# Decoder layer with 32 experts on one core: another expert's gate kept in the spare buffer, and a rebuilt end

## The reference

```python
def moe_ffn(h, w_router, b_router, w_e_gate, b_e_gate, w_e_up, b_e_up, w_e_down, b_e_down):
    ...
    combine = jnp.sum(jax.nn.one_hot(top_idx, N_EXPERTS) * top_w[..., None], axis=1)   # top 4 of 32

    def expert_step(acc, args):
        wg, bg, wu, bu, wd, bd, cw = args
        g = jnp.minimum(xt @ wg + bg, SWIGLU_LIMIT)
        u = jnp.clip(xt @ wu + bu, -SWIGLU_LIMIT, SWIGLU_LIMIT)
        y = ((u + 1.0) * g * jax.nn.sigmoid(SWIGLU_ALPHA * g)) @ wd + bd
        return acc + cw[:, None] * y, None
    ...
x = x + y @ w_out
x = x + moe_ffn(rms_norm(x, g_mlp), ...)
return x
```

## Time and profile before

| | before |
|---|---|
| median of 3 runs | 1132.2 us |
| profiled execution, its own time | 1131.85 us |
| its span, first to last instruction | 1129.9 us |
| PE busy | 1073.4 us (95%) |
| DVE busy | 452.4 us (40%) |
| ACT busy | 170.7 us (15%) |
| POOL busy | 90.1 us (8%) |
| read from HBM | 438.38 MB |
| DMA rate over the span | 389 GB/s |
| weights loaded, expert matrices in full | 4096 KB each, 28.5 to 31.1 us from issue to landing |

### The profile page before, as it was taken

One profiled execution on the slowest core, in us unless ns is written; L12 is line 12 of the kernel. 1 busy time (PEld: TensorE's weight loads), 2 busy tenths in 40 slices (PEclk: granted clock), 3 DMA queues, 4 the chain that ended last, 5 costly groups with the idle time before them and its releaser, 6 DMA issues.

```text
span 1129.9 us, 14464 instructions
## 1 busy us (share of the span) xinstructions
PE 1073.4 (95%) x5719; PEld 510.5 (45%) x5719; DVE 452.4 (40%) x1070; ACT 170.7 (15%) x342; POOL 90.1 (8%) x89
## 2 busy tenths in 40 slices
PE   9999999999999998989889999999899999899998
PEld 7779899843333333333333333333333333233333
DVE  5883666533333333333333333333333233333333
ACT  7546655300000000000000000000000000000000
POOL 3227446000000000000000000000000000000000
PEclk9999999999999999999999999999999999999999
DMA  9836424999999999999999999999999999999996
GB/s 382 361 149 253 195 76 171 421 422 430 427 431 429 432 434 428 432 432 435 427 429 432 430 433 426 431 431 427 431 431 430 427 431 429 431 427 428 427 423 259
DMA packets 27536, 440.09 MB, mean 389 GB/s; under 512 B 3009, under 2 KB 4418, under 8 KB 6114
## 3 DMA queue, kind: packets, MB, share of 16 engines
q1 hardware_dynamic: 26752, 438.71, 91.5%
q10 hardware_dynamic: 738, 0.73, 0.2%
HBM read 438.38 MB, written 1.05 MB: 389 GB/s over the span
## 4 chain that ended last, share of the span: by engine, by line
PE 67%; DMA 30%; DVE 1%; ACT 1%; issue 0%; POOL 0%; DVEq 0%; POOLq 0%
PE bank L1936 40%; DMA ring<-in_w_e_up_dram 30%; PE bank L1901 3%; PE bank L1958 2%; PE bank L1691 1%; PE bank L1921 1%; PE bank L1692 1%; PE bank L1693 1%; PE bank L1980 1%; PE bank L1536 1%; PE bank L1960 1%; PE bank L1778 1%; PE bank L1545 1%; PE bank L1737 1%; PE bank L1779 1%; PE bank L1780 1%
## 5 line engine op out<-in xcount | busy, mean ns | idle before, releaser
L1936 PE MATMUL bank<-ring,heads 128*64 128x512 f32 x3004 | 690.8, 606 | 0.2 <-DVE heads L1335 0.2
L1936 PEld LDWEIGHTS bank<-ring,heads 128*64 128x64 f32 x3004 | 204.0, 138 | 388.4 <-issue 387.8
L1474 DVE TENSOR_TENSOR x<-x,bank 128x512 f32<-128x512 f32 x124 | 79.6, 683 | 145.9 <-PE bank L1960 145.9
L925 ACT ACTIVATE heads<-heads 128x512 f32<-128x512 f32 x32 | 20.2, 630 | 669.6 <-DVE heads L1407 669.6
L1444 DVE SCALAR_TENSOR_TENSOR y_lo<-bank,small,y_hi 128x512 fp32r<-128x512 f32 x31 | 23.3, 750 | 212.5 <-ACT y_hi L921 212.5
L1921 PE MATMUL bank<-bias_parts,e_sel 128*128 128x512 f32 x63 | 32.6, 518 | 46.4 <-DMA ring<-in_w_e_up_dram 42.8
L728 POOL TENSOR_TENSOR x<-x,heads 128x256 f32<-128x256 f32 x2 | 1.4, 726 | 907.7 <-ACT heads L947 907.7
L397 POOL TENSOR_TENSOR w_lo<-ring,w_hi 128x1024 fp32r<-128x1024 f32 (+1 forms) x35 | 65.3, 1890 | 53.6 <-ACT w_hi L751 53.6
L1901 PEld LDWEIGHTS bank<-work,xn 128*128 128x128 f32 x480 | 55.9, 192 | 12.2 <-issue 12.2
L751 ACT ACTIVATE w_hi<-ring 128x512 fp32r<-128x512 f32 (+2 forms) x82 | 57.1, 731 | 23.2 <-PE bank L1780 7.4
L1901 PE MATMUL bank<-work,xn 128*128 128x128 f32 x480 | 60.0, 278 | 0.0
(11 more groups left out here) (315 smaller groups left out, 1030.6 us busy)
## 6 DMA issues: line engine op xcount, KB each, us to landing
ring<-in_w_e_down_dram SPq DMA_DIRECT2D x58, 2048.0 KB, 23.8
ring<-in_w_e_gate_dram SPq DMA_DIRECT2D x24, 4096.0 KB, 28.5
ring<-in_w_e_up_dram SPq DMA_DIRECT2D x24, 4096.0 KB, 31.1
ring<-in_w_e_gate_dram SPq DMA_DIRECT2D x13, 2048.0 KB, 19.4
ring<-in_w_e_up_dram SPq DMA_DIRECT2D x13, 2048.0 KB, 19.3
ring<-in_w_e_down_dram SPq DMA_DIRECT2D x12, 1024.0 KB, 24.0
ring<-in_w_merge_dram SPq DMA_DIRECT2D x4, 2048.0 KB, 8.6
spare<-in_w_e_gate_dram SPq DMA_DIRECT2D x1, 4096.0 KB, 17.9
```

The lines of the kernel that those rows point to most:

```text
L1474: ins = nc.vector.tensor_tensor(x[:, t, 512 * h:512 * h + 512], x[:, t, 512 * h:512 * h + 512], bank67[:, j % 2, :], ALU.add)
L1936: last = mm(bank[C * half:C * half + C, :], lhs(kk), kept_row[half] if kept else w[:, k, 512 * half:512 * half + 512], start=(kk == 0 and ...
```

## The change

Four things are changed together.

1. `spare` holds the gate of expert 3 in place of that of expert 28. The gate of expert 28 is loaded through the ring like others, by the loop. The numbers of the first matrices are given by a table, `FIRST_PLACE`, and `PAIR_ORDER` is turned by one, so that the first seven matrices lie in the pairs that they had. The loop of loads runs ahead by one matrix number: body `it` loads gate it+1, down it, up it+1.
2. At the end the two 2-bank tiles `bank67` and `bank45` are the sums of the output (`FINAL`). PE puts `x` into them by multiplying the identity with it (`add_x`), adds expert 30's rows (`spread_before`, in place of the two scatters) and then expert 31's rows. For expert 31, y is not split: ACT makes the first half of `y_last`, DVE the second, both float32, and the one-hot `last_hotT` is float32 too. ACT and DVE then only copy the sums to `x`, two copies each. POOL has no part in it, and DVE doesn't add expert 30's rows.
3. The last fourth of the last down matrix (half 1, from column 2048 on) is loaded as two transfers of 512 KiB, with a semaphore each.
4. The columns of `w_e_down` are reordered on the host, so that the output is stored by contiguous halves: one transfer of 512 KiB in rows of 2 KiB for c = 0 by SP, and two of 256 KiB for c = 1 by SP and ACT.

```diff
-PAIR_ORDER = (3, 2, 1, 0)
+PAIR_ORDER = (0, 3, 2, 1)
...
-        LAST_BANKS = [[[banks[2], banks[3]], TB], [OB, [banks[0], banks[1]]]]
+        FINAL = [bank67, bank45]
...
+        FIRST_PLACE = {("gate", 0): 1, ("up", 0): 2, ("gate", 1): 3, ("down", 0): 4, ("up", 1): 5, ("gate", 2): 6,
+                       ("down", 1): 7, ("up", 2): 8, ("down", 2): 9, ("up", 3): 10}
+        IN_SPARE = ("gate", STEPS - 1)
...
-                for i in range(2):
-                    part = slice(2048 * i, 2048 * i + 2048)
-                    sp.dma_start(ring[:, s, part], source("down", h, E - 1)[:, part]).then_inc((ring_in[s], last_in[h])[i], 16)
+                for o, n, landed in ((0, 2048, ring_in[s]),) + (((2048, 2048, last_in[0]),), ((2048, 1024, last_in[1]),
+                                                                                        (3072, 1024, last_piece_in)))[h]:
+                    part = slice(o, o + n)
+                    sp.dma_start(ring[:, s, part], source("down", h, E - 1)[:, part]).then_inc(landed, 16)
...
-                sp.dma_start(spare[:, :, :].rearrange("p h n -> p (h n)"), a[ex_src["gate"]][E - STEPS]).then_inc(spare_in, 16)
+                sp.dma_start(spare[:, :, :].rearrange("p h n -> p (h n)"), a[ex_src["gate"]][IN_SPARE[1]]).then_inc(spare_in, 16)
...
                 as_freed("down", 1, "gate", 2)
                 as_freed("up", 2, "down", 1)
-                as_freed("gate", 3, "up", 2)
-                as_freed("down", 2, "gate", 3)
-                as_freed("up", 3, "down", 2)
+                as_freed("down", 2, "up", 2)
+                as_freed("up", 3, "gate", 3)
+                sp.wait_ge(mat_done["down"], 2)
+                load_matrix("gate", STEPS, place_of("gate", STEPS))
+                for h in range(2):
+                    sp.wait_ge((half_done, mat_done)[h]["up"], 3)
+                    load_half("down", h, STEPS - 1, place_of("down", STEPS - 1))
+                sp.wait_ge(mat_done["down"], 3)
+                load_matrix("up", STEPS, place_of("up", STEPS))
...
-                sp.wait_ge(mat_done["up"], prev)
-                load_matrix("gate", e, place_of("gate", u))
-                sp.wait_ge(mat_done["gate"], now)
+                sp.wait_ge(mat_done["up"], now)
+                load_matrix("gate", e_next, place_of("gate", u + 1))
+                sp.wait_ge(mat_done["gate"], following)
                 for h in range(2):
-                    load_half("down", h, e_before, place_of("down", u - 1))
-                sp.wait_ge(mat_done["down"], prev)
-                load_matrix("up", e, place_of("up", u))
+                    load_half("down", h, e, place_of("down", u))
+                sp.wait_ge(mat_done["down"], now)
+                load_matrix("up", e_next, place_of("up", u + 1))
...
-            for u in range(STEPS):
+            for u in range(1, STEPS):
                 expert_body(last_base, u, True)
...
-            for c in range(2):
-                send(sp, c, 0)
+            sp.wait_ge(moved_a, 1)
+            sp.wait_ge(moved_v, 1)
+            sp.dma_start(out[0].rearrange("(t p) n -> p t n", p=P)[:, :, 0:512], x[:, :, 0:512]).then_inc(out_sent, 16)
+            send(sp, 1, 1)
...
+            act.wait_ge(last_down, 1)
+            nc.scalar.activation(y_last[:, 0:256], LAST_DOWN[0][:, 0:256], ACT.Copy, scale=slot_w[:, 1:2]).then_inc(y_kept, 1)
             for c in range(2):
...
+                act.wait_ge(last_spread, c + 1)
+                nc.scalar.activation(x[:, :, 512 * c:512 * c + T], FINAL[c][:, 0, :].rearrange("p (t n) -> p t n", t=NT),
+                                     ACT.Copy).then_inc(moved_a, 1)
...
-            add_rows(last_base + (STEPS - 2))
+            dve.wait_ge(last_down, 2)
+            nc.vector.tensor_scalar(y_last[:, 256:512], LAST_DOWN[1][:, 256:512], slot_w[:, 1:2], None, ALU.mult).then_inc(y_by_vector, 1)
...
+                dve.wait_ge(last_spread, c + 1)
+                nc.vector.tensor_copy(x[:, :, 512 * c + T:512 * c + 2 * T],
+                                      FINAL[c][:, 1, :].rearrange("p (t n) -> p t n", t=NT)).then_inc(moved_v, 1)
...
+            def add_x(c):
+
+                for h in range(2):
+                    for t in range(NT):
+                        mm(FINAL[c][:, h, T * t:T * t + T], ident[:, :], by_half(t)[:, h, c, :], start=t == 0, stop=False)
...
+            def spread_before(c):
...
+                for t in range(NT):
+                    for y in (y_hi, y_lo):
+                        for h in range(2):
+                            mm(FINAL[c][:, h, T * t:T * t + T], hotT[C * h:C * h + C, t, :], y[C * h:C * h + C, T * c:T * c + T],
+                               start=False, stop=False)
             last_piece(4)
+            pe.wait_ge(rows_added, (last_base + (STEPS - 2)) * 2)
+            add_x(0)
...
             last_piece(5)
+            pe.wait_ge(hotT_made, total)
+            pe.wait_ge(ehT_made, total)
+            add_x(1)
...
                 if h == 1:
-                    scatter(it - 1, 1)
+                    spread_before(1)
...
                 if h == 0:
-                    scatter(it - 1, 0)
+                    spread_before(0)
+            pe.wait_ge(last_piece_in, 16)
             for c in range(2):
...
+                last_product(1, 3, c).then_inc(last_down, 1)
...
                 for t in range(NT):
                     for h in range(2):
...
+                        last = mm(FINAL[c][:, h, T * t:T * t + T], last_hotT[C * h:C * h + C, t, :], y_last[C * h:C * h + C, T * c:T * c + T],
+                                  start=False, stop=t == NT - 1)
+                last.then_inc(last_spread, 1)
```

More of the change, by code:

```diff
@@ L248, in build @@
         hotw = work[:, 640:896].rearrange("p (t u s) -> p t u s", t=NT, u=2)
-        by_pool = [hb(2560 + 256 * i, 256) for i in range(2)]
+        y_last = e_g
         combT = work[0:E, 1152:1408].rearrange("p (t q) -> p t q", t=NT)
@@ L415, in adds @@
         def adds(n):
-            if n == place_of("down", 0):
+            if n == 0:
+                return 0, 0
+            if n == FIRST_PLACE["down", 0]:
                 return 32, 32
@@ L428, in count_at @@
             if in_last:
-                landed += 16 * (n // 4 + 1)
+                landed += 16 * (n // 4 + 1 + (n % 4 == 3) - (h == 1 and n % 4 in (1, 3)))
             return landed + base * (PER_GROUP[h] // STEPS)
@@ L436, in col, with by_half @@
             return ap.unsqueeze(2).to_broadcast([ap.shape[0], ap.shape[1], n])
-        xo = x[:, :, :].rearrange("p t (h c n) -> p t h c n", h=2, c=2)
+        def by_half(t):
+            return x[:, t, :].rearrange("p (c h n) -> p h c n", c=2, h=2)
         def send(eng, c, t):
[L442 to L448, removed]
+            eng.wait_ge(moved_a, c + 1)
+            eng.wait_ge(moved_v, c + 1)
+            eng.dma_start(out[0, P * t:P * t + P, 512 * c:512 * c + 512], x[:, t, 512 * c:512 * c + 512]).then_inc(out_sent, 16)
         @block.sync
@@ L571, in expert_body @@
                 e = sp.snap(sp.to_reg(it & (E - 1)), min_val=0, max_val=E - 1)
-                e_before = sp.snap(sp.to_reg((it - 1) & (E - 1)), min_val=0, max_val=E - 1)
-                now, prev = sp.to_reg(it), sp.to_reg(it - 1)
                 if last:
[L575 to L578, removed]
+                    e_before = sp.snap(sp.to_reg((it - 1) & (E - 1)), min_val=0, max_val=E - 1)
+                    now, prev = sp.to_reg(it), sp.to_reg(it - 1)
+                    for h in range(2):
+                        sp.wait_ge((half_done, mat_done)[h]["up"], prev)
+                        load_half("gate", h, e, place_of("gate", u))
                     if ends:
@@ L610, in _ @@
                     sp.wait_ge(turned, N_UNITS)
-                    load_half("gate", 1, 0, 0)
+                    load_half("gate", 1, 0, FIRST_PLACE["gate", 0])
                 if name == "cv1":
@@ L1914, in product @@
                     s = slots_of(n)[h]
-                    halves = isinstance(base, int) or m == "down" or in_last
+                    halves = in_first or m == "down" or (in_last and n not in (-1, 1))
                     by = h if halves else 0
```

105 lines of the change are left out of this document (42 added, 63 removed).

## The result

The changed kernel takes 1138.2 us (median of 5 runs, 1137.89 to 1138.32); the kernel before took 1132.39 in the same comparison. The ratio is 1.0045 with a 95% interval of 1.0033 to 1.0056, which is 3.7 to 6.3 us slower. (The ratio is estimated over all runs and is not the quotient of the two medians, which lie 5.8 us apart.) The forecast was 1137.2, 5.0 us slower.

What follows compares the result with a forecast made beforehand. The weight stream paces the long middle, PE bounds the end. Late up 31 1.4, x on PE 3.5 and tail 0.1 sum to 5.0 us: profiled 1131.85 becomes 1136.9, median 1137.2; forecast's own range 1135.4 to 1139.0, overall 1133.2 to 1139.2.

Steps and rivals of the forecast that it cites:

- The hole: Queue runs empty from about 308 us until down 2 frees its slot and up 4 is issued at 309.55.
- S: Time the queue loses around up 4, delaying landings from down 27 on: 4.4 us, bounds 3.5 to 5.5.
- 2 MiB row: Trace row for loading on an empty queue: 8.1 us issue to landing, 4.9 for bytes, 3.2 fixed.
- next to nothing: Spare time at gate 5, issued at 318.76: lands at 331.7 by itself against 332.3 behind up 4.
- The room: Time from a load's landing to PE's first use: 6.6 us at up 28, 3.0 at up 31, the tightest.
- No load holds it after that: Behind up 31 PE waits for no load, since added PE work comes ahead of down 31.
- x by PE: Two add_x runs around down 30's second half add 3.5 us to PE's path, bounds 1.8 to 3.8.
- rival of one record per matmul: The x matmuls cost 1.8 us in place of 3.5, total 3.3 us slower, 1135.5; chance 8%.
- The tail: Last product to span's end: X + 7.1 against X + 6.96 before, so +0.1 us (-0.6 to +0.9).
- X: End of PE's last product: 1122.94 before, forecast at about 1127.8.
- The first rival: Queue does not run empty at 308, S near 0: +0.6 us, 1132.8; chance 14%.
- The third: Slower PE clock after a wait at up 31 adds 1.6 us, 1138.8; at up 28 made up; chance 12%.

Runs made afterwards that it cites:

- refill: Changed kernel, but gate 28 is loaded into the spare behind down 3, its ring load cut to 64 KB: 1136.39 us, ratio 1.0031 to the kernel before.
- ring_only: Kernel before with only the new spare and order of loads (gate 3 in the spare), its end unchanged: 1136.93 us, ratio 1.0036 to the kernel before.
- no_x: Changed kernel without the eight matmuls that add x on PE, so its output is incomplete: 1135.77 us, ratio 1.0020 to the kernel before.
- end_only: Kernel before with only the new end (x by PE, halved last transfer, contiguous output), loads as before: 1136.49 us, ratio 1.0034 to the kernel before.
- x_early: Changed kernel with the first add_x moved ahead of up 31's first use, in two halves: 1136.86 us, ratio 1.0033 to the kernel before.

## Why the prediction came out right, and where its sizes were off

**What bounds.** As read: the stream sets the pace of the middle, and at the end PE is ahead or behind by what is left of the room at up 31. The trace after has the load of up 31 on the chain. That step held.

**The hole.** It is where the forecast put it, and refill shows that it is the cause. Its size S was taken as 4.4 and is 6.0 by the landing of up 31 (1101.8 against 1095.8), outside my bounds of 3.5 to 5.5. The landing of up 4 itself came out as forecast, 322.4 for 322.5, but by two errors that cancel. The fixed cost of the restart was less than I took: 4 MiB landed 12.1 us after issue, 2.3 more than the 9.75 for their bytes, not 3.2. And up 4 was issued 0.8 us later (310.32 against 309.55), in which single executions differ. The Trainium skill's figure of about 2.0 us ("DMA: Bandwidth & Descriptors", section on the anatomy of one DMA), which stands there for transfers that GpSimd issues while these are SP's, is nearer to this row than the 2 MiB row that I preferred. The loss that I worked out from it, 3.0, is still further from 6.0 than 4.4 was.

What I had no term for is what follows the restart. The landings of up 4 (issued at 309.55) and gate 5 (at 318.76) in the kernel before:

```profile
ring<-in_w_e_up_dram SPq DMA_DIRECT2D x1, 4096.0 KB, 18.7
ring<-in_w_e_gate_dram SPq DMA_DIRECT2D x1, 4096.0 KB, 19.2
```

Up 4 landed at 328.2 there, so the changed kernel's stream was still 5.8 us ahead, a loss of 4.0. Then gate 5, issued at 319.54, lands at 334.0, 11.6 behind up 4 and not 9.75: 1.85 more, where I had "next to nothing". At gate 5 the lead is 4.0 us (334.0 against 338.0), and from up 6 on (384.2 against 387.5) it stays at 3.3 to 3.5, looked at as far as 590 us. In ring_only gate 5 came 13.5 us behind up 4, in no_x 11.5, and both have up 6 at 384.1 to 384.2 too. Windows of 5 us from 320 and 330 have 390 and 372 GB/s, where before had 436 and 419. So the step that failed in size is "with next to nothing to spare" behind gate 5: of the loss, some 4 us came at up 4 and some 2 more over the loads up to up 6. Why these come late, no run shows. The missing bytes alone say 5.4 us.

**The room.** The two places came out as S less the room: at up 31 it is 6.0 - 3.0 = 3.0, measured +3.04; at up 28 it is 6.0 - 6.6 = -0.6, measured 1028.41 against 1028.99. The rule was right and only S was mis-sized: +3.0 where the sum had +1.4. The room of "some 3 us" that the forecast gave the last fourth of down 31 was misread: by its own numbers that fourth lands at 1124.2 and PE comes to it at some 1125.9 (1120.99 before, and 4.9 later). Measured were 1125.2 and 1127.89, so there was room in any case and nothing hung on it.

**Waits behind up 31.** "No load holds it after that" held in the changed kernel: its only waits for loads from 985 us on are four for up and one for gate. It held because of x. Without x, or with the old end, down 31 is late as well (no_x, ring_only). The forecast named this cover rightly, but did not say what the ring costs without it.

**x by PE.** 3.75 us against 3.5 (0.46 to 0.48 us for one float32 matmul of 256 columns, where the earlier trace rows gave 0.43). The rival of one record per matmul falls: the records are eight each time. Its full price shows where PE waits for nothing (end_only, 3.79); in the changed kernel it is worth 2.4 (no_x), since it stands in part in the time of the waits that the hole makes.

**spread_before.** The scatters' 0.66 us have become 0.67 (1124.68 to 1125.35): 0, as taken.

**The tail.** X + 6.83, taken as X + 7.1. The steps came as worked out: the spread ends at X + 2.3 (2.4), the first store is issued at X + 2.2 (2.25). The difference is the rate of the stores, 381 to 387 GB/s: the forecast had X + 7.4 for the old rate and X + 6.85 for a faster one, and took about the middle.

**Sum and rivals.** The terms were 1.4 + 3.5 + 0.1 = 5.0; measured they are 3.0 + 3.9 - 0.2 = 6.7 between the two profiled executions. The medians differ by 5.8, and the ratio's interval allows 3.7 to 6.3. That 5.0 comes so near to the ratio's 5.1 is in part luck: the profiled execution of the kernel before (1131.85), on which the forecast built, was faster than all five of its runs in the comparison (1132.13 to 1135.57), and this hides part of what the first term lacks. The first rival, no empty queue, falls. The third, a fall of the clock at the end, did not cost there: behind the wait of 1.24 us at up 31 the clock stayed. It came where the forecast said that it would be made up, at up 28, in ring_only and no_x (waits of 3.0 us, then 3.51 and 3.15 us for eight records in place of 1.94). In the changed kernel's profile the wait at up 28 was 1.44 us, not some 3, and no fall followed it. The Trainium skill's warning ("TensorE: Matmul & The Clock Gate", section on HAM oscillation) says that waits for a next slice bring the slow clock again and again. The traces agree for the longer waits only, 24 of 31 of 2.16 us or more, and not for each of them (counts below).

## What to carry to other kernels

A ring that is full by count can have an empty queue: what matters is when the next slot comes free against when the queued bytes run out. An issue 0.6 us ahead of the last landing (ring_only) was no better than one 1.1 us behind it. Taking a matrix out of the stream early gives little lead if the ring can't be refilled in that time (3.3 of 9.75 us here); the lead is lost while the queue waits for the slot's release and in the loads right behind it, and the price appears where the room is smallest, here 790 us later. Work moved to PE to relieve an engine that is not late costs its full time wherever PE sets the end, and two such edits may cost less together than the sum of both alone, since one stands in the other's waits.

## What the runs showed of the hardware

- The queue did not end sharply. From 306 to 309, just before the last landing at 309.2, the DMA share was 0.73, 0.46 and 0.04, though the loads in it were not done.
- 4 MiB on the queue as it ran empty took 12.1 us in the changed kernel, 12.0 in ring_only and 12.1 in no_x.
- The price of the hole did not hang on the last landing. In the changed kernel up 4 was issued 1.1 us after it, in ring_only 0.6 us ahead of it (309.83 against 310.4). In ring_only too the DMA share had fallen to 0.35, 0.08 and 0.04 over the 3 us from 307 to 310. Gate 7 landed at 393.8 to 393.9 in both and in no_x, against 397.2 before: of the lead of 9.75 us only 3.3 to 3.4 were left.
- Falls of the clock went with the longer waits, but not surely. From 610 to 1030 us the profiles of before, after, ring_only and no_x have 31 waits of PE for a load of 2.16 to 4.08 us. Behind 24 of them the next eight products took 2.6 to 3.7 us in place of 1.94; behind 7 (2.17 to 3.01 us) they took 1.94. Behind no wait of 1.82 us or less was there a fall.
- In x_early the granted clock was 0.50, the 1.2 GHz level, from 1028 to 1032: in the last 1.2 us of a wait of 3.56 us and in the first products behind it, which took 3.68 us in place of 1.94.
- Stores of rows of 2 KiB ran at 381 and 387 GB/s in the two full windows of 1 us (1133 to 1135), those of 1 KiB in the kernel before at 335, 348 and 344 (1126 to 1129), of which the earlier trace rows is the middle one.
